# A layer's gate products and the later attention projections as pairs of seven half-width products, with the input's sums stored over the input's own buffer

## The reference, cut to what matters

```python
proj = rmsnorm(x, norm_mix_g) @ w_in
q_m, k_m, v_m, if_pre, o_pre, q_a, k_a, v_a, gate_pre = jnp.split(proj, ...)
...
g_a, g_b = jnp.split(jax.nn.sigmoid(gate_pre), 2, axis=-1)
merged = g_a * (y_a @ w_proj_a) + g_b * (y_b @ w_proj_b)
x = x + merged @ w_out
```

## Time and profile before

| | |
|---|---|
| median of 3 runs | 1911.19 us (1910.96 to 1911.21) |
| span of the profiled execution | 1909.1 us |
| own time of the profiled execution | not listed apart; the runs lie 2.1 us above its span |
| PE / PEld busy | 1898.5 us (99%) / 1591.0 us (83%) |
| DVE / ACT / POOL busy | 1255.4 / 735.3 / 265.1 us (66 / 39 / 14%) |
| matmuls 128x512 (L1561 to L1563) | 5820 |
| matmuls 128x256 (L1637 to L1639) | 2352 |
| chain that ended last | PE 94%, DVE 3%, ACT 1%, POOL 1% |

### The profile page before, as it was taken

One profiled execution on the slowest core, in us unless ns is written; L12 is line 12 of the kernel. 1 busy time (PEld: TensorE's weight loads), 2 busy tenths in 40 slices (PEclk: granted clock), 3 DMA queues, 4 the chain that ended last, 5 costly groups with the idle time before them and its releaser, 6 DMA issues.

```text
span 1909.1 us, 26308 instructions
## 1 busy us (share of the span) xinstructions
PE 1898.5 (99%) x10599; PEld 1591.0 (83%) x10599; DVE 1255.4 (66%) x1894; ACT 735.3 (39%) x1265; POOL 265.1 (14%) x156
## 2 busy tenths in 40 slices
PE   9999999999999999999999999999999999999998
PEld 7788888888888888999997778877777878899998
DVE  7777543345455748777776756766776667887874
ACT  6332322233334444344435522224444354444442
POOL 0211210111111113000004001121111133100002
PEclk9999999999999999999999999999999999999999
DMA  5322233232321323233333222322121322333332
GB/s 177 102 70 85 88 86 115 89 99 67 89 67 45 115 91 104 78 106 102 114 108 103 77 67 78 100 79 65 56 67 40 116 79 87 100 100 100 100 130 81
DMA packets 53472, 172.77 MB, mean 90 GB/s; under 512 B 5963, under 2 KB 10643, under 8 KB 53352
## 3 DMA queue, kind: packets, MB, share of 16 engines
q1 hardware_dynamic: 52912, 170.66, 28.8%
q10 hardware_dynamic: 440, 0.44, 0.1%
HBM read 168.86 MB, written 2.22 MB: 90 GB/s over the span
## 4 chain that ended last, share of the span: by engine, by line
PE 94%; DVE 3%; ACT 1%; POOL 1%; issue 0%; DVEq 0%
PE PS L1561 22%; PE PS L1563 22%; PE PS L1562 22%; PE PS L1637 5%; PE PS L1639 5%; PE PS L1638 5%; PE PS L1983 1%; PE PS L2005 1%; PE PS L1780 1%; PE PS L1795 1%; PE PS L1961 1%; PE PS L1841 1%; PE PS L1827 1%; PE PS L1818 1%; PE PS L1748 1%; POOL XT L3338 1%
## 5 line engine op out<-in xcount | busy, mean ns | idle before, releaser
L1561 PE MATMUL PS<-HH,WH 128*128 128x512 f32 x1124 | 444.0, 395 | 0.8 <-DVE WL L2467 0.7
L1563 PE MATMUL PS<-HH,WL 128*128 128x512 f32 x1124 | 438.0, 390 | 0.0
L1562 PE MATMUL PS<-HL,WH 128*128 128x512 f32 x1124 | 437.4, 389 | 0.0
L2064 ACT ACTIVATE WH<-RAW 128x1024 fp32r<-128x1024 f32 (+2 forms) x256 | 261.1, 1020 | 336.4 <-PE PS L1563 271.4
L2467 DVE TENSOR_TENSOR WL<-RAW,WH 128x1024 fp32r<-128x1024 f32 (+2 forms) x195 | 251.2, 1289 | 113.7 <-ACT WH L2064 112.0
L1561 PE MATMUL PS<-AH,WH 128*128 128x512 f32 x816 | 323.7, 397 | 0.0
L1563 PE MATMUL PS<-AH,WL 128*128 128x512 f32 x816 | 318.1, 390 | 0.0
L1562 PE MATMUL PS<-AL,WH 128*128 128x512 f32 x816 | 317.6, 389 | 0.0
L1561 PEld LDWEIGHTS PS<-HH,WH 128*128 128x128 f32 x1124 | 211.1, 188 | 49.7 <-issue 4.2
L1563 PEld LDWEIGHTS PS<-HH,WL 128*128 128x128 f32 x1124 | 211.0, 188 | 45.1
L1562 PEld LDWEIGHTS PS<-HL,WH 128*128 128x128 f32 x1124 | 211.2, 188 | 42.2 <-issue 0.2
(11 more groups left out here) (360 smaller groups left out, 2260.7 us busy)
## 6 DMA issues: line engine op xcount, KB each, us to landing
RAW<-wst SPq DMA_DIRECT2D x292, 512.0 KB, 3.6
RAW<-wst SPq DMA_DIRECT2D x16, 256.0 KB, 2.6
RAW<-wst SPq DMA_DIRECT2D x8, 384.0 KB, 3.1
XT<-xT SPq DMA_DIRECT2D x3, 512.0 KB, 7.3
out<-XT SPq DMA_DIRECT2D x4, 384.0 KB, 2.5
AR<-mx SPq DMA_DIRECT2D x4, 256.0 KB, 6.2
AR<-scr SPq DMA_DIRECT2D x16, 64.0 KB, 4.3
AR<-scr SPq DMA_DIRECT2D x8, 128.0 KB, 4.8
```

Of the source, the lines that this page charges most:

```text
L1561: T.matmul(out, wh, XH[:, k, :], start=k == 0, stop=False)
L1562: T.matmul(out, wh, XL[:, k, :], start=False, stop=False)
L1563: m = T.matmul(out, wl, XH[:, k, :], start=False, stop=k == nk - 1)
L2064: t = A.activation(whole(WH, i, n), raw(i)[:, 0:n], ACT.Copy, scale=1.0)
```

## The change

The eight `ga`, the eight `gb` and eight of the nine units of each of the head pairs 1 to 3 become pairs: 20 pairs, 40 units. The code calls them MIXED. `ga` and `pa` now come two by two.

- Each MIXED pair has its chunks in the order 0, 2, 4, 6, 1, 3, 5. The subtractions of all seven chunks and two of the four additions are done by POOL; two additions stay on DVE.
- `Stream` takes the place of `Fill` for `ga`/`pa` and for the fillers of attention: steps of one chunk product, or a quarter of a single unit. 32 steps go with the blocks of each of head pairs 0 to 2, and 28 with those of head pair 3.
- The recombination is `pair_keep` (ACT), `pair_middle`, `pair_sum` (DVE) and then a second operation per unit, `pair_out` (DVE), which multiplies by the norm's factor. PSUM bank 4 holds the first bank of a pair during attention.
- The input's sums are made in the last two mLSTM heads (`t_sums` DVE, `t_hi` ACT, `t_lo` POOL); the high parts TXH lie over the input XT, the low parts TXL in new room of SBUF. After the last use `reload_x` loads XT again.

```diff
+PAIR_ORDER = (0, 2, 4, 6, 1, 3, 5)
+ADD_ON_POOL = (5, 6)
...
-    for j in range(8):
+    for j in range(0, 8, 2):
         add("ga", j)
+        add("ga", j + 1)
         add("pa", j)
+        add("pa", j + 1)
...
+def mixed_pairs():
+
+    starts = [AT["ga", j, 0] for j in range(0, 8, 2)] + [AT["gb", j, 0] for j in range(0, 8, 2)]
+    starts += [AT["qa", hp, 0] + x for hp in (1, 2, 3) for x in (0, 2, 4, 6)]
+    return {p + n: p for p in starts for n in (0, 1)}
...
         if p is None:
             user[x] = [("lo", i)]
         else:
-            user[x] = [("lo", i, 4), ("lo", i, 5), ("added", i, 6)] if p == i else [("lo", p, 2), ("lo", p, 6)]
+            last = 3 if i in MIXED else 2
+            user[x] = [("lo", i, 4), ("lo", i, 5), ("added", i, 6)] if p == i else [("lo", p, last), ("lo", p, 6)]
...
+class Stream:
...
+        self.chunks = [(i, c) for i in range(at, end + 2) for c in ([None] if pair_start(i) is None else
+                                                                    PAIR_ORDER if pair_start(i) == i else [])][ready:]
...
+    def prepare(self):
+        e = self.e
+        while self.chunks and all(self.done.get(y, -1) < self.n for y in W_BEFORE[self.chunks[0]]):
+            while self.n_add < min(2, len(self.chunks)):
+                e.chunk_add(*self.chunks[self.n_add])
+                self.n_add += 1
+            self.n_add -= 1
+            y = self.chunks.pop(0)
+            e.chunk_hi(*y)
+            e.chunk_lo(*y)
+            if y[0] >= self.end:
+                break
+
+    def step(self):
+        e, (kind, i, x) = self.e, self.steps[self.n]
+        if kind == "pair":
+            if x == 0:
+                e.load(i + 5)
+                e.load(i + 6)
+            if x == 0 and len(e.ring) == 2:
+                e.hold(4, "sum_z", i)
+            elif x in (0, 1, 2):
+                e.sum_bank("sum" if x else "sum_z", i + (x == 2))
+            e.pair_products("1", i, x)
...
+        now, self.queue = self.queue, []
+        for i2, y in now:
+            e.pair_out(i2, y)
...
+        self.prepare()
...
+            if x == 0:
+                e.pair_keep(i)
+            elif x == 6:
+                e.pair_middle(i)
+            elif x in (3, 5):
+                e.pair_sum(i, int(x == 3))
+                self.queue.append((i, int(x == 3)))
...
-    for j in range(8):
-        unit(e, unit_of("ga", j))
-        unit(e, unit_of("pa", j))
+    stream = Stream(e, unit_of("ga", 0), unit_of("gb", 7) + 1, 4)
+    for _ in range(60):
+        stream.step()
...
+            def reload_x(s):
+                sp.wait_ge(*at("prod", unit_of("gb", 6), 3))
+                for g in range(4):
+                    d = S.dma_start(XT[:, 2 * g:2 * g + 2, :], xT_d[:, 2 * g:2 * g + 2, :])
...
+                if sfx == "1":
+                    for m in range(4):
+                        pe.wait_ge(*at("t_lo", m))
...
+                        T.matmul(out, wh[:, w], XH[:, k, x], start=m == 0, stop=False)
+                        T.matmul(out, wh[:, w], XL[:, k, x], start=False, stop=False)
+                        t = T.matmul(out, wl[:, w], XH[:, k, x], start=False, stop=m == 3)
...
+            def pair_middle(s, i):
...
+                dve.wait_ge(*at("prod", i, 6))
+                dve.wait_ge(*at("kept", i))
+                V.tensor_tensor(held[:, 0:256], z[:, 256:512], kept[:, 0:256], ALU.add).then_inc(
...
+                t = V.tensor_tensor(held[:, 256:512], z[:, 0:256], held[:, 0:256], ALU.add)
+                t.then_inc(*bank_read.next("free", "sum_z", i))
...
+                    t = V.tensor_tensor(dst, src, rb, ALU.mult)
+                t.then_inc(*dve_done["attn"].next("out", u))
...
-                if c not in LO_ON_POOL:
+                if i not in MIXED:
                     return
                 pool.wait_ge(*at("hi", i, c))
                 t = G.tensor_tensor(chunk(WL, i, c), raw_chunk(i, c), f(chunk(WH, i, c)), ALU.subtract)
...
+            def chunk_add(s, i, c):
+                if i not in MIXED or c not in ADD_ON_POOL:
+                    return
+                r1, r2 = raw(i), raw(i + 1)
+                pool.wait_ge(*at("added", i, 4))
+                if c == 5:
+                    pool.wait_ge(*at("lo", i, 1))
+                    t = G.tensor_tensor(r1[:, 512:1024], r1[:, 512:1024], r1[:, 0:512], ALU.add)
+                else:
+                    pool.wait_ge(*at("lo", i, 2))
+                    t = G.tensor_tensor(r2[:, 0:512], r1[:, 0:512], r2[:, 512:1024], ALU.add)
```

More of the change, by code:

```diff
@@ L198, in place_weights @@
         elif p == i:
-            chunks = [((i, c), (h + c,), ("prod", i, c)) for c in range(7)]
+            order = PAIR_ORDER if i in MIXED else range(7)
+            chunks = [((i, c), (h + n,), ("prod", i, c)) for n, c in enumerate(order)]
         else:
@@ L305 @@
     small_products = small_evict = small_select = keep_warm = gates_products = gates_evict = gates_select = none
+    t_sums = t_hi = t_lo = pair_middle = pair_sum = pair_out = reload_x = none
     pair_products = pair_keep = pair_held = pair_add = pair_silu = pair_hi = pair_lo = none
@@ L652, in mlstm @@
         e.weights(h)
-        fill.quarters(12 if h else 8)
+        if h == 3:
+            e.t_sums(1)
+        fill.quarters(6 if h else 8)
+        if h == 3:
+            e.t_hi(1)
+            e.t_lo(1)
+        fill.quarters(6 if h else 0)
         for t in range(4):
@@ L798, in pair_steps @@
         if p == i:
-            steps += [("pair", i, c) for c in range(7)]
+            steps += [("pair", i, c) for c in (PAIR_ORDER if quarters else range(7))]
+        elif p is None and quarters:
+            steps += [("unit", i, range(2 * q, 2 * q + 2)) for q in range(4)]
         elif p is None and nk == 6:
@@ L2084, in pair_keep, with t_hi, pair_out @@
                 act.wait_ge(*at("prod", i, 0))
-                last = [x for x in range(i - 3, i) if pair_start(x) == x]
+                last = [x for x in range(i - 5, i) if pair_start(x) == x]
                 if last:
-                    act.wait_ge(*at("free", "sum", last[0]))
-                t = A.activation(KEPT[:, 0:256], PS[:, s.bank["sum_z", i], 0:256], ACT.Copy, scale=1.0)
+                    act.wait_ge(*at("free", "sum", last[-1]))
+                if i in MIXED:
+                    act.wait_ge(*(at("scored", 3, 3) if UNITS[i][0] == "ga" else at("unit", unit_of("pa", 7))))
+                t = A.activation(temps(i)[0][:, 0:256], PS[:, s.bank["sum_z", i], 0:256], ACT.Copy, scale=1.0)
                 t.then_inc(*act_done["ffn"].next("kept", i))
+            def t_hi(s, m):
+                act.wait_ge(*at("t_sums", m))
+                act.wait_ge(*at("gates", "sum"))
+                t = A.activation(TXH[:, m:m + 5:4, :], T_SUM.rearrange("p (x t) -> p x t", x=2), ACT.Copy, scale=1.0)
+                t.then_inc(*act_done["attn"].next("t_hi", m))
+            def pair_out(s, i, n):
+                if UNITS[i][0] in ("ga", "gb"):
+                    act.wait_ge(*at("out", i + n))
+                    x = gate_tile(i + n)
+                    A.activation(x, x, ACT.Tanh, scale=0.5).then_inc(*act_done["attn"].next("tanh", i + n))
             def pair_silu(s, i, n):
@@ L2111, in norm_root @@
                 if gone:
-                    act.wait_ge(*at("free", "sum", unit_of(*gone)))
+                    act.wait_ge(*at(*evicted(unit_of(*gone))))
                 act.wait_ge(*at("mean", norm))
```

226 lines of the change are left out of this document (199 added, 27 removed).

## The result

The changed kernel takes 1991.11 us (four runs, 1990.66 to 1992.46) against 1911.09: 1.042 times as long, interval 1.0405 to 1.0435. That is 80 us more; I had put 1948, 37 more, with a range of 1908 to 1966. The profiled execution has a span of 1988.9 us and itself took 1990.66.

The account below looks back on a forecast made before the run. PE was taken to bound the kernel before, the load-to-POOL loop attention after the change. Span 1909.1 - 4.0 (ga) + 40.9 (attention) = 1946.0, plus 2.1 around it: 1948 us, range 1908 to 1966.

Parts of the forecast that it names:

- clock or longer detours: Whole kernel: a falling clock or longer waits than forecast put the time above 1966 us; chance 0.09.
- attention up to the first L: Attention's start until the first pair's last POOL subtraction, which frees a RAW buffer for the next load: 10.8 us.
- 12 loops inside head pairs: Attention, from one pair's buffer release to the next: four loops of 18.1 us and eight of 16.8.
- 3 loops at a head pair's end: Attention, buffer release to release across a head pair's end: three loops of 24.8 us, 74.4 together.
- behind the last L: Attention's end: only one last product follows the last pair's buffer-freeing subtraction, 1.4 us.
- (a): Attention's ordinary loop: DVE and POOL slow each other, adding 1.4 us to the bare 15.4, loop 16.8.
- (b): Each head pair's first pair boundary: ACT's rounding waits behind scores, maxima, exponentials and evictions; loop 18.1 us, once per head pair.
- (c): Head pair's end: a single va unit and block work delay the next pair's chunks; loop 24.8 us, three times.
- no wait: The ga part: POOL has chunk weights ready 2 to 3 us early, so the pairs save 4.0 us.
- 102 us: Sign that the forecast is right: the ga and pa stretch takes this long.
- The gain of a pair: PE: seven products instead of two single units save 1.01 us a pair, 20.2 us over 20 pairs.
- The rival of a falling clock: PE's new idle times lower the clock and products cost up to double: above 1960 us; 0.09 shared with longer detours.

Follow-up runs that it names:

- e14: Changed kernel with DVE's pair_out of attention's units cut to 8 of 512 columns: 1984.7 us.
- e5: Changed kernel with the maxima and exponentials of a block two steps of products later in the queues: 1972.1 us.
- e16: Changed kernel with 28 steps shared among five points instead of seven, so head pair 3's blocks come every 5.6 steps instead of 4: 1995.6 us.
- e17: Changed kernel with the eight gb units single as before and the input loaded again earlier: 1968.6 us.
- e1: Changed kernel with pairs in ga alone, attention's units single, and the input loaded again earlier: 1920.1 us.
- e9: Pairs in ga alone, with the score bias transfers moved behind the loads of the second and third pair: 1912.7 us.
- e8: Changed kernel with the last product of attention's sixteen pairs computed twice, 22.6 us more PE work at full clock: 1987.8 us.
- e7: Changed kernel with a fourth RAW buffer, additions behind pair_middle and pair_sum, and later maxima and exponentials: 1938.3 us.
- e10: e7 with the bias transfers later and ACT's copy of the first product ahead of the roundings: 1934.3 us.
- e2: Changed kernel with a fourth RAW buffer during attention, over two unused AL blocks: 1972.2 us.

## Why the prediction was wrong

The bound and the mechanism were right, the sum was half of what came: the time fell into the case that I had called "clock or longer detours" and given 0.09. By its terms, in us:

| term | forecast | measured |
|---|---|---|
| `ga`/`pa` | -4.0 | +2.5 |
| attention up to the first L | 10.8 | 10.6 |
| 12 loops inside head pairs | 206.8 | 225.5 |
| 3 loops at a head pair's end | 74.4 | 83.5 |
| behind the last L | 1.4 | 8.7 |
| behind attention | 0 | +1.6 |
| whole span against before | +36.9 | +79.8 |

- **(a), the loop of 16.8 us:** right. Five of the loops are 16.3 to 16.7, and the chain shows the steps with nearly the forecast's durations. That DVE and POOL slow each other is there too (1.42 us in the mean for 1.29), and e14 gives it some 1 us a bare loop where I had put 1.4.
- **(b), the step that failed: "once in each head pair".** I let the exponentials stand ahead of a rounding in one loop of four, 18.1 us, and gave the others 16.8. In head pair 0 no inner loop is long, in head pairs 1 and 2 two of three are (17.7 to 19.6), and in head pair 3 every one (29.4, 18.7, 18.9). The last I did not look at at all: I used one loop table for all head pairs, though the front part says that `gb` fills head pair 3 and the code shares 28 steps among seven points. e5, which took the block's operations out of the chunks' way, shortened most of these loops; e16 and e17 place the rest in head pair 3. Of the 18.7 us too few, 15.3 lie in head pair 3, and the 29.4 loop alone is 11.3 over its 18.1.
- **(c):** the right place, 9.1 us too small over three. It was put together of bare durations; e5 brings these loops to 24.2 to 25.7, near the 24.8 of the sum, so a good part was again what stands in ACT's and DVE's queues. By the chain, 3.8 us of the three are matmuls of the single unit at the low clock.
- **The end:** I let one product follow the last subtraction (692.3). But PE had waited 3.4 us for ACT's copy of the last pair's first product, until 690.0, and then had five products and work of the block left.
- **`ga`, "no wait":** wrong. The sum looked at POOL alone and left out SP's queue, in which the bias transfers stood. e1 and e9 show 7.4 us of it in the kernel with `ga` pairs only. The 102 us that I gave as a sign for `ga` and `pa` came from the row that begins too early, and should have read 83.
- **The gain of a pair, 1.01 us:** a little too large. It took the distance of matmuls from the feed-forward pairs; here it is 0.86 (last section), 3.0 us less over 20 pairs.
- **The rival of a falling clock** named a time above 1960, and the clock did fall. It is a minor part: by the chain some 11 of the 80 us, and e8, with the clock higher and more work, took nearly the same time.
- **Sums of the input, `reload_x`:** no cost was found. In e9, which has both, the time is that of before within 0.2%.
- **The weighing of the DMA page** ("DMA: Bandwidth & Descriptors" of the Trainium skill, Anatomy of one DMA): the section gives 2.0 us and the bytes by 436 GB/s for transfers that GpSimd issues, and these loads are issued by SP, so it did not bear on them directly. The loads in the chains take 3.4 to 3.6 us, nearer the row's 3.6 than the 3.2 that I worked out, and neither would have changed the outcome.

What stays open: why 4 to 5 us of waits remain in each of head pairs 1 and 2 in e7. Over attention, PE's waits in e7 and e10 are spread over ten causes and more, and no run took them apart.

## What to carry to other kernels

When an operand that was prepared far ahead is now prepared just in time, write down the loop from a buffer's release to its next release, and add to each step everything that stands ahead of it in its engine's queue, for every stage separately: here engines that were busy for 40 to 60% of the time set the pace. Removing one wait of such a loop can tell little (19 and 4 us) while the next queue holds the same work; try them together (36). And where PE idles at a low clock, give it more work for one run: if the time stays, that work is not on the path. What the clock costs has to be read apart, from the matmuls at the lower level that stand in the chain.

## What the runs showed of the hardware that I had not expected

The matmuls of 256 columns follow each other a little more slowly here than in the feed-forward pairs. Changed, first and 24th matmul of the first `ga` pair:

```profile
282.96 0.28 PE L1811 MATMUL PS<-HH,WH 128*128 128x256 f32 x1
...
285.71 0.29 PE L1813 MATMUL PS<-TXH,WL 128*128 128x256 f32 x1
```

23 distances in 2.75 us are 0.1196 us each, against 0.1178 from the earlier trace rows; over some 1100 distances at the full clock in attention the mean is 0.1197. A pair then saves 0.86 us and not 1.01, 17.2 of 20.2 in all. What the cause is no run tells.

DVE's addition of two SBUF operands took 1.70 us next to POOL's subtractions (e2, above) and 0.70 alone: 1.0 longer, in line with the exclusive lock that "SBUF — State Buffer" of the Trainium skill (SBUF: two separate sides) describes. And in e8 22.6 us of added matmuls left the time within 3 us of changed, while the granted clock in attention rose from 0.90 to 0.96.
